# Three low parts of weights per layer made by GpSimd, and softmax divisions written as products of two tensors

## The chip, the core and the metric

The kernel runs on one core of a Trainium2 chip. The metric is the device time of one execution in microseconds, the median of several. The engines are TensorE (PE in the profile), VectorE (DVE), ScalarE (ACT), GpSimd (POOL) and SyncE (SP), which issues the loads of the weights. They run beside each other and wait for each other on semaphores.

## What is computed

Two transformer blocks of two layers each, on one sequence of 256 tokens and 1024 features, in fp32. The change lies in the heads of the first block's layers:

```python
def hybrid_layer(x, ...):
    proj = rms_norm(x, ln1) @ w_in
    ...
    y_moba = moba_attention(mq, mk, mv)      # 6 heads; causal softmax over 256 keys at this length
    ...
    h = mlstm_chunkwise(...)                 # 4 heads
    h = h * sigmoid(xo)
    y_mlstm = rms_norm(h, mlstm_norm)
    ...
    y_swa = swa_attention(sq, sk, sv, swa_sinks)   # 6 query heads, window 128, softmax with a sink
    x = x + concatenate([y_moba, y_mlstm, y_swa]) @ w_out
    u = rms_norm(x, ln2) @ w_up
    return x + square(relu(u)) @ w_down
```

## The kernel before

Every weight is multiplied as the sum of two parts in a short fp32 format, so that the product keeps its precision. The weights come in units of up to 128x1024 elements, two to a slab of 1 MB, in the order in which TensorE uses them. For each unit ScalarE writes the high part (`act_split`, line 377) and VectorE the low part, the weight less its high part (`dve_split`, line 386, a TENSOR_TENSOR with both inputs in SBUF). High and low parts lie in rings of RING = 4 buffers: unit u reuses the buffers of unit u - 4, and ScalarE waits until TensorE has used those. The semaphore `unit_lo` counts the low parts in the order of the units. TensorE waits on it before each unit (`pe_unit_in`), and SyncE before it overwrites a slab (three slab buffers).

Each engine has its own program in an order that is written out by hand. In a layer of the first block, five groups of projection columns come first. Then u0 is the number of the next unit, and a loop `for i in range(0, N1, 2)` runs over the 16 heads in pairs: heads 0 to 3 are mLSTM, 4 to 9 MOBA, 10 to 15 the windowed attention. Units u0 to u0+3 are the last column group (the values), u0+4 to u0+7 the first half of the output projection (a chunk pair each, consumed inside the loop from i = 8 on), u0+8 and later its second half.

One pass of the loop does, on TensorE: the transposes of the scaled probabilities of heads i and i+1 (line 1016, after `prob_ready`), the scores of heads i+4 and i+5 (line 1000), the products with the values of heads i-2 and i-1 (line 1048), and column products or chunks of the output projection (lines 420 to 422). At i = Y_TURN = 10 it also transposes the mLSTM output, after `y_ready`. On VectorE: `first` for heads i+4 and i+5 (line 1444: scores plus mask from PSUM, with the row maximum; these wait for the scores), at i = 10 the low part of the mLSTM output (line 1560), `seconds(i + 2)` (line 1457: the reciprocal of the sums, for the heads with a sink after adding the sink at line 1454; line 1460: four instructions that scale the probabilities of heads i+2 and i+3, of 128 and 256 columns a head), `pair(i - 2)` (line 1468), the low part of one weight unit, and at i = 4 and i = 6 the mLSTM output's normalisation (`y_first`, lines 1477 to 1483, and `y_mean`, lines 1489 and 1491). On ScalarE: copies of the transposes, high parts, the exponentials (line 887).

GpSimd follows the mLSTM output (`pool_layer1`): gate (line 1690), square (1693), then the wait for `y_mean`, the root (`root`, line 1658), a product with the root (1698) and one with the gain (1702), which sets `y_ready`.

Of the kernel before, what the change touches and what calls it, by code (L numbers as in the profile page):

```python
# [8 lines left out]
F32 = mybir.dt.float32  # L9
# [4 lines left out]
P = 128  # L14
# [12 lines left out]
MOBA, LSTM, SWA, SWA_KV = 6, 4, 6, 2  # L27
# [36 lines left out]
HALF = 1024  # L64
SLAB = 2 * HALF
RAW, RING = 3, 4
# [16 lines left out]
def wide_units(name, c0, w):  # L83

    n = HALF // w
    while DC % n or (DC // n) % 2:
        n -= 1
    return [[(name, k + i, c0, w) for i in range(n)] for k in range(0, DC, n)]


def tile_units(name, chunks, c0):

    return [[(name, k, c0, P) for k in range(a, min(a + DC, chunks))] for a in range(0, chunks, DC)]
# [3 lines left out]
G1 = [(0, ZLQ + LSTM * HD)]  # L97
# [4 lines left out]
def plan1():  # L102
    plan = []
    for c0, w in G1:
        plan += wide_units("w_in", c0, w)
    for k in range(0, DC, 2):
        plan.append([("w_out", c, n * P, P) for c in (k, k + 1) for n in range(OUT_HALF)])
    for n in range(OUT_HALF, DC):
        plan += tile_units("w_out", DC, n * P)
    for n in range(FC1):  # L110
        plan += tile_units("w_up", DC, n * P)
    for n in range(DC):
        plan += tile_units("w_down", FC1, n * P)
    return plan
# [26 lines left out]

PLAN = [(l, unit) for l in range(DEPTH) for unit in plan1()] + [(l, unit) for l in range(DEPTH) for unit in plan2()]
SLABS = len(PLAN) // 2
DOWN1, DOWN2 = len(tile_units("", FC1, 0)), len(tile_units("", FC2, 0))


def width_of(u):
    return sum(b[3] for b in PLAN[u][1])
# [26 lines left out]
def build(nc, a, out):  # L175
    ctx = ExitStack()
    with ctx:
# [16 lines left out]
        raw = [sb(f"raw{i}", [P, SLAB]) for i in range(RAW)]  # L194
        w_hi = [sb(f"w_hi{i}", [P, HALF], F32R) for i in range(RING)]
        w_lo = [sb(f"w_lo{i}", [P, HALF], F32R) for i in range(RING)]
# [30 lines left out]
        rinv = sb("rinv", [P, PROBS, T])  # L227
# [81 lines left out]
        prob = [work[:, i * GROUP:(i + 1) * GROUP] for i in range(PROBS)]  # L309
# [71 lines left out]
        def dve_split(dve, b, to):  # L381
            while b.made < min(to, len(PLAN)):
                u = b.made
                n, j = width_of(u), u // 2
                dve.wait_ge(s["unit_hi"], u + 1)
                nc.vector.tensor_tensor(w_lo[u % RING][:, 0:n], raw[j % RAW][:, (u % 2) * HALF:(u % 2) * HALF + n],  # L386
                                        w_hi[u % RING][:, 0:n].bitcast(F32), ALU.subtract).then_inc(s["unit_lo"], 1)
                b.made += 1

# [74 lines left out]
        def pool_squares(pool, b):  # L466

            k = b.at("rsum")
            for n in range(1, DC):
                pool.wait_ge(s["sq_ready"], k * DC + n + 1)  # L470
                if n > 1:
                    pool.wait_ge(s["sq_added"], k * (DC - 1) + n - 1)
                nc.gpsimd.tensor_tensor(sumsq[:, :], sumsq[:, :], sq[n % 2][:, :], ALU.add).then_inc(s["sq_added"], 1)
# [40 lines left out]
        def pool_norm(pool, b):  # L514
            n = b.mark("rsum")
            pool.wait_ge(s["ms_ready"], n)
            nc.gpsimd.tensor_tensor(rstd[:, :], ms2[:, :], half[:, 0:T], ALU.pow).then_inc(s["rstd_ready"], 1)  # L517
# [815 lines left out]
        def dve_layer1(dve, b, l, next_gain):  # L1333
# [115 lines left out]
            def seconds(i):  # L1449
                hd, p = HEADS1[i], i % PROBS  # L1450
                wait(dve, value(b, "exp_done", hd["n"] + 2))
                total = esum
                if hd["sink"] is not None:
                    tick(dve, b, dve_chain, nc.vector.tensor_tensor(tot[:, p:p + 2, :], esum[:, p:p + 2, :],
                                                                    esink[:, p:p + 2, :], ALU.add))
                    total = tot
                tick(dve, b, dve_chain, nc.vector.reciprocal(rinv[:, p:p + 2, :], total[:, p:p + 2, :]))
                for j in (p, p + 1):
                    for t in range(T):
                        ins = nc.vector.tensor_scalar(prob[j][:, HALVES1[t]], prob[j][:, HALVES1[t]],  # L1460
                                                      rinv[:, j, t:t + 1], None, ALU.mult)
                    ins.then_inc(s["prob_ready"], 1)

            def pair(i):
# [22 lines left out]
            def y_mean():  # L1487
                wait(dve, value(b, "y_sq", 1))
                tick(dve, b, dve_chain, nc.vector.tensor_reduce(ssq[:, m0:m1].rearrange("p (t h) -> p t h", t=T),
                                                                by_head(lstm_q[:, :, :]), X, ALU.add))  # L1490
                nc.vector.tensor_scalar(msq[:, m0:m1], ssq[:, m0:m1], 1.0 / HD, EPS, ALU.mult, ALU.add)\
                    .then_inc(s["qms_ready"], 1)
# [57 lines left out]
            for i in range(0, N1, 2):  # L1550
                if i == 0:
                    lstm_probs(2)
                    lstm_probs(3)
                if i + PROBS < N1:
                    first(i + PROBS)
                    first(i + PROBS + 1)
                if i == Y_TURN:
                    bank = f["y"][0]
                    wait(dve, value(b, "y_hi", 1))
                    nc.vector.tensor_tensor(act_b[:, 3:5, 1, :], tp[bank][:, :].rearrange("p (c s) -> p c s", s=S),  # L1560
                                            act_b[:, 3:5, 0, :].bitcast(F32), ALU.subtract).then_inc(s["y_lo"], 1)
                if LSTM <= i + 2 < N1:
                    seconds(i + 2)
                if i - 2 >= LSTM:
                    pair(i - 2)
                if i <= Y_TURN:
                    dve_split(dve, b, u0 + RING - 1 + i // 2)
                if i == LSTM:
                    y_first()
                if i == LSTM + 2:  # L1570
                    y_mean()
            dve_split(dve, b, u0 + RING + Y_TURN // 2 + 1)
            pair(N1 - 2)
            gain = pcol1[:, l, C_LN2:C_LN2 + DC]
# [58 lines left out]
            dve_down(dve, b, DOWN1, 1.0, act_a, next_gain)  # L1633

        def pool_layer1(pool, b, l):
            pool_norm(pool, b)
            if l == 0:
                pool.wait_ge(s["const_in"], 16 * n_const)
# [52 lines left out]
                .then_inc(s["y_gated"], 1)  # L1691
            wait(pool, value(b, "y_gated", 1))
            nc.gpsimd.tensor_tensor(lstm_q[:, :, :], lstm_h[:, :, :], lstm_h[:, :, :], ALU.mult).then_inc(s["y_sq"], 1)
            m0, m1 = R1_AT[2], R1_AT[2] + T * LSTM
            root(3, m0, m1)
            wait(pool, value(b, "qrs_ready", 3))
# [3 lines left out]
            wait(pool, value(b, "y_unit", 1))  # L1700
            g = prow1[:, l, R_MN:R_MN + LSTM * HD].unsqueeze(1).broadcast_to([P, T, LSTM * HD])
            nc.gpsimd.tensor_tensor(lstm_h[:, :, :], lstm_h[:, :, :], g, ALU.mult).then_inc(s["y_ready"], 1)
            pool_squares(pool, b)
            pool_norm(pool, b)
            layer_over(b, LAYER1)
# [540 lines left out]
```

## Time and profile before

| | us |
|---|---|
| Median of 3 runs | 1725.83 (1723.84 to 1726.46) |
| The profiled execution | 1721.79 |
| Its span, first to last instruction | 1720.0 |
| TensorE busy | 1672.9 (97%) |
| VectorE busy | 1257.4 (73%) |
| ScalarE busy | 991.0 (58%) |
| GpSimd busy | 147.3 (9%) |

TensorE's granted clock was 1.0 (2.4 GHz) throughout. In the rows, PE is TensorE's products and PEld its weight loads, L1460 is line 1460, `out<-in` are the program's names, and a time in square brackets is the engine's idle time before the row with what ended it. A timeline's row may stand for several like instructions (x4): its length then runs from the start of the first to the end of the last. Instructions of one engine overlap a little, so from start to start is shorter than the length. The first layer's head stage lies at 76 to 127 us, that of the second layer at 377 to 427.

### The profile page before, as it was taken

To read this page: it belongs to the slowest core of one execution; us is meant where nothing else is said; L and a number is where in the kernel's file an instruction comes from. 1 tells how busy PE (TensorE), PEld (TensorE's weight loads), DVE (VectorE), ACT (ScalarE), POOL (GpSimd) and SP (SyncE) were. 2 spreads that over 40 slices of the span, in tenths; PEclk is the share of its full clock that TensorE was granted. 3 is DMA by queue.
4 is the path that set the end of the run, shared out by engine and by line. 5 is a ranking of instruction groups with operands and counts; after the bars stand their busy time and mean duration, and the time that the engine had idled before them with its cause. 6 is when DMAs were issued, how large, how long until landed. Compare 5 with 4: busy or idle time off the path is not lost.

```text
span 1720.0 us, 25627 instructions
## 1 busy us (share of the span) xinstructions
PE 1672.9 (97%) x9966; PEld 1448.4 (84%) x9966; DVE 1257.4 (73%) x2025; ACT 991.0 (58%) x1664; POOL 147.3 (9%) x100
## 2 busy tenths in 40 slices
PE   7989999998999999999999999999999999999999
PEld 5778888877888888888877988888888787898888
DVE  7777766767776568876777878767886767778874
ACT  5666654567665455554566665545555466665552
POOL 2611000161100000001300000000000220000000
PEclk9999999999999999999999999999999999999999
DMA  7525555532655555556423455555556542355553
GB/s 283 190 99 184 196 197 196 219 136 99 233 196 200 195 193 196 187 205 245 172 99 123 178 190 196 193 201 194 188 183 217 208 183 99 139 181 196 183 203 129
DMA packets 62023, 313.99 MB, mean 183 GB/s; under 512 B 22685, under 2 KB 24353, under 8 KB 25294
## 3 DMA queue, kind: packets, MB, share of 16 engines
q1 hardware_dynamic: 60382, 303.93, 49.9%
q0 software_dynamic: 1232, 4.22, 0.8%
q10 hardware_dynamic: 288, 4.19, 0.6%
q8 instruction: 80, 1.31, 0.3%
q14 instruction: 41, 0.34, 0.1%
HBM read 311.25 MB, written 7.36 MB: 185 GB/s over the span
## 4 chain that ended last, share of the span: by engine, by line
PE 88%; DVE 6%; ACT 4%; issue 2%; DMA 0%; SPq 0%; ACTq 0%; DVEq 0%
PE acc L411 44%; PE acc L413 23%; PE acc L400 4%; PE acc L401 4%; PE acc L402 4%; DVE w_lo L386 2%; ACT w_hi L377 2%; PE acc L420 1%; PE acc L422 1%; PE acc L421 1%; PE sc L783 1%; PE acc L808 1%; PE tp L794 1%; ACT work L887 1%; PE tp L1016 1%
## 5 line engine op out<-in xcount | busy, mean ns | idle before, releaser
L386 DVE TENSOR_TENSOR w_lo<-raw,w_hi 128x1024 fp32r<-128x1024 f32 (+1 forms) x564 | 685.0, 1221 | 290.5 <-ACT w_hi L377 288.7
L377 ACT ACTIVATE w_hi<-raw 128x1024 fp32r<-128x1024 f32 (+1 forms) x564 | 584.1, 1039 | 194.2 <-PE acc L413 120.2
L411 PE MATMUL acc<-act_a,w_hi 128*128 128x512 f32 x1440 | 506.9, 396 | 1.2 <-DVE w_lo L386 1.2
L411 PE MATMUL acc<-hidden,w_hi 128*128 128x512 f32 x1216 | 421.8, 391 | 0.0
L413 PE MATMUL acc<-act_a,w_lo 128*128 128x256 f32 x1440 | 402.2, 279 | 0.0
L413 PE MATMUL acc<-hidden,w_lo 128*128 128x256 f32 x1216 | 340.0, 280 | 0.0
L411 PEld LDWEIGHTS acc<-act_a,w_hi 128*128 128x128 f32 x1440 | 269.7, 187 | 68.1 <-issue 8.5
L413 PEld LDWEIGHTS acc<-act_a,w_lo 128*128 128x128 f32 x1440 | 271.7, 189 | 0.1
L411 PEld LDWEIGHTS acc<-hidden,w_hi 128*128 128x128 f32 x1216 | 227.5, 187 | 50.3
L585 ACT COPY part<-acc 128x256 f32<-128x256 f32 x272 | 101.4, 373 | 270.9 <-PE acc L413 269.9
L411 PE MATMUL acc<-act_b,w_hi 128*128 128x512 f32 x688 | 239.4, 392 | 0.0
L413 PEld LDWEIGHTS acc<-hidden,w_lo 128*128 128x128 f32 x1216 | 229.6, 189 | 0.0
L413 PE MATMUL acc<-act_b,w_lo 128*128 128x256 f32 x688 | 192.7, 280 | 0.0
L411 PEld LDWEIGHTS acc<-act_b,w_hi 128*128 128x128 f32 x688 | 128.7, 187 | 28.3
L400 PE MATMUL acc<-w_hi,act_a 128*128 128x512 f32 (+2 forms) x352 | 135.2, 384 | 17.0 <-DVE w_lo L386 17.0
L401 PE MATMUL acc<-w_lo,act_a 128*128 128x512 f32 (+2 forms) x352 | 131.6, 374 | 0.0
L402 PE MATMUL acc<-w_hi,act_a 128*128 128x512 f32 (+2 forms) x352 | 131.6, 374 | 0.0
L413 PEld LDWEIGHTS acc<-act_b,w_lo 128*128 128x128 f32 x688 | 130.0, 189 | 0.1
L517 POOL TENSOR_TENSOR rstd<-ms,neg_half 128x2 f32<-128x2 f32 x10 | 12.5, 1251 | 1183.1 <-DVE ms L508 1183.1
L400 PEld LDWEIGHTS acc<-w_hi,act_a 128*128 128x128 f32 x352 | 67.3, 191 | 32.6 <-issue 15.5
L436 ACT ACTIVATE act_a<-x_res,pcol 128x256 fp32r<-128x256 f32 x64 | 31.8, 507 | 104.8 <-DVE x_res L599 92.5
L402 PEld LDWEIGHTS acc<-w_hi,act_a 128*128 128x128 f32 x352 | 67.3, 191 | 11.7
(210 smaller groups left out, 2043.8 us busy)
## 6 DMA issues: line engine op xcount, KB each, us to landing
raw<-in_slabs SPq DMA_DIRECT2D x282, 1024.0 KB, 4.8
na_skew<-in_rpb SPq DMA_DIRECT2D x32, 128.0 KB
na_bias<-na_skew ACTq DMA_DIRECT2D x2, 2048.0 KB, 8.6
t_skew<-t_by_distance POOLq DMA_DIRECT2D x2, 1024.0 KB, 14.3
t_bias<-t_skew POOLq DMA_DIRECT2D x1, 2048.0 KB, 10.7
x_res<-in_x SPq DMA_DIRECT2D x1, 1024.0 KB, 4.9
out_x<-x_res SPq DMA_DIRECT2D x8, 128.0 KB, 4.8
prow<-in_prow SPq DMA_DIRECT2D x1, 518.0 KB
```

Source lines behind the costliest of these rows:

```text
L377: nc.scalar.activation(w_hi[u % RING][:, 0:n], raw[j % RAW][:, (u % 2) * HALF:(u % 2) * HALF + n], ACT.Copy).then_inc(s["unit_hi"], 1)
L386: nc.vector.tensor_tensor(w_lo[u % RING][:, 0:n], raw[j % RAW][:, (u % 2) * HALF:(u % 2) * HALF + n], w_hi[u % RING][:, 0:n].bitcast(F32), ...
L400: nc.tensor.matmul(to, xh, wh, start=first and i == 0, stop=False)
L401: nc.tensor.matmul(to, xh, wl, start=False, stop=False)
L402: mm = nc.tensor.matmul(to, xl, wh, start=False, stop=last and i == n - 1)
L411: nc.tensor.matmul(bank[:, :], wh, src[:, c + i, :, :].rearrange("p i s -> p (i s)"), start=first and i == 0, stop=False, skip_group_check ...
L413: mm = nc.tensor.matmul(bank[:, S:2 * S], wl, src[:, c + i, 0, :], start=False, stop=last and i == n - 1, skip_group_check=True)
L420: nc.tensor.matmul(to, wh, src[:, c, 0, :], start=first, stop=False, skip_group_check=True)
L421: nc.tensor.matmul(to, wh, src[:, c, 1, :], start=False, stop=False, skip_group_check=True)
L422: return nc.tensor.matmul(to, wl, src[:, c, 0, :], start=False, stop=last, skip_group_check=True)
L436: nc.scalar.activation(to[:, n, 0, :], x[:, n, :], ACT.Identity, scale=gain[:, n:n + 1])\
L585: nc.scalar.copy(part[n % 2][:, :], acc[bank][:, 0:S]).then_inc(s["part_ready"], 1)
```

## The change

Three low parts per layer, of units u0+5, u0+6 and u0+7, are made by GpSimd (`pool_split`): u0+5 behind the square at line 1693 and ahead of the root, u0+6 and u0+7 behind the product with the gain. Each waits for its high part and for the low parts of all units ahead of it, so that `unit_lo` still counts in order. VectorE makes low parts in the loop for i up to 4 only; behind the loop it waits once for `unit_lo` (`dve_skip`) and goes on with u0+8. And the scaling of the probabilities is a TENSOR_TENSOR with the reciprocals broadcast over the columns in place of a TENSOR_SCALAR. It has two inputs in SBUF, in place of one and a scalar pointer. The diff:

```diff
--- before.py
+++ after.py
@@ -141,6 +141,7 @@
 
 PLAN = [(l, unit) for l in range(DEPTH) for unit in plan1()] + [(l, unit) for l in range(DEPTH) for unit in plan2()]
 SLABS = len(PLAN) // 2
+UNITS1 = len(plan1())
 DOWN1, DOWN2 = len(tile_units("", FC1, 0)), len(tile_units("", FC2, 0))
 
 
@@ -387,6 +388,20 @@
                                         w_hi[u % RING][:, 0:n].bitcast(F32), ALU.subtract).then_inc(s["unit_lo"], 1)
                 b.made += 1
 
+        def pool_split(pool, u):
+
+            n, j = width_of(u), u // 2
+            pool.wait_ge(s["unit_hi"], u + 1)
+            pool.wait_ge(s["unit_lo"], u)
+            nc.gpsimd.tensor_tensor(w_lo[u % RING][:, 0:n], raw[j % RAW][:, (u % 2) * HALF:(u % 2) * HALF + n],
+                                    w_hi[u % RING][:, 0:n].bitcast(F32), ALU.subtract).then_inc(s["unit_lo"], 1)
+
+        def dve_skip(dve, b, to):
+
+            while b.made < to:
+                b.made += 1
+            dve.wait_ge(s["unit_lo"], to)
+
 
 
         def columns_unit(u, src, c, banks, w, first, last):
@@ -1457,8 +1472,9 @@
                 tick(dve, b, dve_chain, nc.vector.reciprocal(rinv[:, p:p + 2, :], total[:, p:p + 2, :]))
                 for j in (p, p + 1):
                     for t in range(T):
-                        ins = nc.vector.tensor_scalar(prob[j][:, HALVES1[t]], prob[j][:, HALVES1[t]],
-                                                      rinv[:, j, t:t + 1], None, ALU.mult)
+                        w = HALVES1[t].stop - HALVES1[t].start
+                        ins = nc.vector.tensor_tensor(prob[j][:, HALVES1[t]], prob[j][:, HALVES1[t]],
+                                                      rinv[:, j, t:t + 1].broadcast_to([P, w]), ALU.mult)
                     ins.then_inc(s["prob_ready"], 1)
 
             def pair(i):
@@ -1563,12 +1579,13 @@
                     seconds(i + 2)
                 if i - 2 >= LSTM:
                     pair(i - 2)
-                if i <= Y_TURN:
+                if i <= LSTM:
                     dve_split(dve, b, u0 + RING - 1 + i // 2)
                 if i == LSTM:
                     y_first()
                 if i == LSTM + 2:
                     y_mean()
+            dve_skip(dve, b, u0 + RING - 1 + Y_TURN // 2)
             dve_split(dve, b, u0 + RING + Y_TURN // 2 + 1)
             pair(N1 - 2)
             gain = pcol1[:, l, C_LN2:C_LN2 + DC]
@@ -1633,6 +1650,7 @@
             dve_down(dve, b, DOWN1, 1.0, act_a, next_gain)
 
         def pool_layer1(pool, b, l):
+            u0 = l * UNITS1 + sum(len(wide_units("", c0, w)) for c0, w in G1[:G_V])
             pool_norm(pool, b)
             if l == 0:
                 pool.wait_ge(s["const_in"], 16 * n_const)
@@ -1691,6 +1709,7 @@
                 .then_inc(s["y_gated"], 1)
             wait(pool, value(b, "y_gated", 1))
             nc.gpsimd.tensor_tensor(lstm_q[:, :, :], lstm_h[:, :, :], lstm_h[:, :, :], ALU.mult).then_inc(s["y_sq"], 1)
+            pool_split(pool, u0 + RING + LSTM // 2 - 1)
             m0, m1 = R1_AT[2], R1_AT[2] + T * LSTM
             root(3, m0, m1)
             wait(pool, value(b, "qrs_ready", 3))
@@ -1700,6 +1719,8 @@
             wait(pool, value(b, "y_unit", 1))
             g = prow1[:, l, R_MN:R_MN + LSTM * HD].unsqueeze(1).broadcast_to([P, T, LSTM * HD])
             nc.gpsimd.tensor_tensor(lstm_h[:, :, :], lstm_h[:, :, :], g, ALU.mult).then_inc(s["y_ready"], 1)
+            for u in range(u0 + RING + LSTM // 2, u0 + RING - 1 + Y_TURN // 2):
+                pool_split(pool, u)
             pool_squares(pool, b)
             pool_norm(pool, b)
             layer_over(b, LAYER1)
```

## Rows read from the trace of the kernel before

**Rows 1.** The page: the chain that ended last, share of the span by engine.
```profile
PE 88%; DVE 6%; ACT 4%; issue 2%; DMA 0%; SPq 0%; ACTq 0%; DVEq 0%
```
**Rows 2.** TensorE's waits, 76 to 127 us, then 380 to 430: total, times, longest.
```profile
PE tp L1016 <- DVE work L1460: 4.9, 4, 1.6
...
PE tp L1016 <- DVE work L1460: 4.7, 4, 1.5
```
**Rows 3.** Timeline of TensorE, layer 1: start, length, line, operation, count, idle before it.
```profile
100.72 1.00 PE L1016 MATMUL tp<-ident,work 128*128 128x128 f32 x6 [1.51 <-DVE work L1460]
101.66 0.93 PE L1000 MATMUL sc<-heads_t 64*128 64x128 f32 x8
...
106.65 0.55 PE L1016 MATMUL tp<-ident,work 128*128 128x128 f32 x3 [1.63 <-DVE work L1460]
108.12 0.55 PE L1016 MATMUL tp<-ident,work 128*128 128x128 f32 x3 [0.93 <-DVE work L1460]
...
113.19 1.00 PE L1016 MATMUL tp<-ident,work 128*128 128x128 f32 x6 [0.85 <-DVE work L1460]
...
114.92 0.39 PE L420 MATMUL acc<-act_b,w_hi 128*128 128x256 f32 x1
```
**Rows 4.** Timeline of VectorE, layer 1.
```profile
100.12 1.01 DVE L1460 TENSOR_SCALAR work<-work,rinv 128x128 f32<-128x128 f32 x4
101.04 0.42 DVE L1468 TENSOR_TENSOR act_b<-acc,act_b 128x256 fp32r<-128x256 f32 x1
101.38 1.22 DVE L386 TENSOR_TENSOR w_lo<-raw,w_hi 128x1024 fp32r<-128x1024 f32 x1
...
103.71 0.35 DVE L1444 CUSTOM_DVE_ANT_0 work<-sc,mask_s,neg_sink 128x128 f32<-128x128 f32 x1 [0.32 <-issue]
...
105.47 2.59 DVE L1460 TENSOR_SCALAR work<-work,rinv 128x128 f32<-128x128 f32 x4
...
111.58 0.69 DVE L1560 TENSOR_TENSOR act_b<-tp,act_b 128x512 fp32r<-128x512 f32 x1 [0.47 <-ACT act_b L1279]
```
**Rows 5.** Timeline of GpSimd, layer 1.
```profile
80.42 2.36 POOL L1680 TENSOR_TENSOR qk<-qk,qk_b 128x1024 f32<-128x1024 f32 x1
...
98.87 1.04 POOL L1693 TENSOR_TENSOR lstm_q<-lstm_h 128x512 f32<-128x512 f32 x1
103.47 1.65 POOL L1658 TENSOR_TENSOR rstd_h<-msq,neg_half 128x8 f32<-128x8 f32 x1 [3.57 <-DVE msq L1491]
105.20 1.04 POOL L1698 TENSOR_TENSOR lstm_h<-lstm_h,rstd_h 128x512 f32<-128x512 f32 x1
106.32 1.39 POOL L1702 TENSOR_TENSOR lstm_h<-lstm_h,prow 128x512 f32<-128x512 f32 x1
```
**Rows 6.** Timelines: GpSimd and VectorE near 1361 us, VectorE near 72 and 60 us.
```profile
1361.04 9.01 POOL L2079 TENSOR_TENSOR na_bias<-mask_n,na_bias 128x4096 f32<-128x4096 f32 x1 [2.95 <-DMA na_bias<-na_skew]
...
1361.19 9.94 DVE L386 TENSOR_TENSOR w_lo<-raw,w_hi 128x1024 fp32r<-128x1024 f32 x1 [1.67 <-ACT w_hi L377]
...
72.55 0.67 DVE L1403 TENSOR_TENSOR qk<-z,rope_gc 128x384 f32<-128x384 f32 x1
...
59.82 1.49 DVE L1403 TENSOR_TENSOR qk<-z,rope_gc 128x384 f32<-128x384 f32 x3
```
**Rows 7.** Timeline of VectorE, near 375 us: a product of 128 columns.
```profile
374.85 0.28 DVE L1403 TENSOR_TENSOR qk<-z,rope_gc 128x128 f32<-128x128 f32 x1
```
**Rows 8.** Timelines of short stretches: single instructions of GpSimd and VectorE.
```profile
406.18 1.10 POOL L1698 TENSOR_TENSOR lstm_h<-lstm_h,rstd_h 128x512 f32<-128x512 f32 x1
406.30 1.13 DVE L1460 TENSOR_SCALAR work<-work,rinv 128x256 f32<-128x256 f32 x1
...
106.51 1.29 DVE L1460 TENSOR_SCALAR work<-work,rinv 128x128 f32<-128x128 f32 x1
```
**Rows 9.** Timelines of VectorE and TensorE, layer 2 of the first block.
```profile
404.33 0.35 DVE L1444 CUSTOM_DVE_ANT_0 work<-sc,mask_s,neg_sink 128x128 f32<-128x128 f32 x1
...
408.85 0.55 PE L1016 MATMUL tp<-ident,work 128*128 128x128 f32 x3 [0.82 <-DVE work L1460]
```

## Prediction

> **What bounds the kernel now.** I read the chain that ended last first [rows 1]: 88% of it is TensorE, so a change outside TensorE counts only where TensorE waits. Then the waits of TensorE in the heads' stage of each layer of the first block [rows 2]: of this change's neighbourhood nearly all of the waiting, 4.9 us in the first layer and 4.7 us in the second, is for the scaled probabilities of line 1460. Then the timelines of the stage. On TensorE [rows 3] one sees the transposes of heads 8 and 9 at 100.72, of 10 at 106.65, of 11 at 108.12 and of 12 and 13 at 113.19, each started by VectorE. On VectorE [rows 4]: head pair 8/9 scaled at 100.12, a weight unit's low part at 101.38 (two more follow, one after pair 10/11 and one after 12/13), the row maxima of heads 12 and 13 at 103.71, and pair 10/11 scaled at 105.47 in 2.59 us where pair 8/9 took 1.01. On GpSimd [rows 5]: the mLSTM output's square at 98.87, the root at 103.47, its two products at 105.20 and 106.32. Those 2.59 us lie exactly beside those products. The weight units are not late: the first moved one, u0+5, is wanted at 114.92 [rows 3].
>
> **Who holds whom.** In the second block's layer 2 a 128x4096 product on GpSimd starts at 1361.04 and takes 9.01; a VectorE low part that starts 0.15 later takes 9.94 instead of 1.22 [rows 4, 6]. It ran after GpSimd, not beside it: 1361.19 + 9.94 - 1.22 = 1369.91, or 0.14 ahead of GpSimd's end. That is a TENSOR_TENSOR with both inputs in SBUF, the form the divisions now take. A factor that is broadcast doesn't free the instruction: the 128x384 product with rope_gc, which is broadcast over the heads, took 0.67 at 72.55 beside GpSimd's last rope products, and three others of its shape 1.49, some 0.5 each [rows 6]. So I take it that GpSimd and a two-input VectorE instruction exclude each other for a whole instruction, and that who asks first goes first: GpSimd's 406.18 product slipped in behind one VectorE instruction, and the next, at 406.30, took 1.13 [rows 8].
>
> The Trainium skill, page SBUF — State Buffer, section Who interferes with whom, has this as a rule: tensor_tensor with two SBUF inputs contends with GpSimd's reads just as a 2-port tensor_scalar does, and the one that issues first blocks the other fully. It speaks against the new form being any cure, and the trace agrees by the 9.94 us.
>
> **Part 1, the form of the division.** Start to start, a product of 128 columns costs 0.21 (0.28 busy [rows 7]) and of 256 columns 0.34 (101.04 to 101.38 [rows 4, 7]): 1.10 for a pair of heads, where the tensor_scalars need 0.92 (100.12 to 101.04). So +0.09 for the first head and +0.18 for both, wherever a pair is on the path. Pairs 4/5 and 6/7 are covered by the column products of a value unit, which TensorE has ahead of either pair's transposes (lines 1130 and 1131); uncovered they would cost 0.18 each. The bounds of such a pair are +0.0 and +0.4 (its four instructions at 0.07 to 0.1 more each).
>
> The Trainium skill, page VectorE: DVE Perf Modes, section The perf-mode tier table, gives 1227 ns for a fp32 tensor_scalar of 2048 columns and 2293 ns for a tensor_tensor. By that the 384 columns of a head would cost 0.20 more, not 0.09, and an estimate by it would add some 0.1 to each layer; the rows of these very sizes are nearer.
>
> **Part 2, unit u0+5 on GpSimd, behind the square.** VectorE is rid of 1.22 [rows 4] between pair 4's low part and the mean at line 1489. GpSimd gains an instruction whose price no row has; the nearest is 128x1024 with two inputs, 2.36 [rows 5], and 9.01 / 4 = 2.25 bounds it below; if it must alternate with VectorE it grows by what it waits. I take 2.36. In layer 1 it is issued at 98.87 + 1.04 + 0.08, plus 0.18 for part 1: 100.17. VectorE starts its first product at 100.12, so GpSimd comes in behind it (100.33), and ends at 100.17 + 2.36 + 0.16 = 102.69, letting go 0.15 earlier. The three other products of pair 8/9 wait: head 8 is ready at 102.95 (before: 100.66), head 9 at 103.5 (101.13). Head 9's transpose, and with it the scores that start at 101.66, move by 2.37. The row maxima start 0.14 behind those scores' end: 104.96 + 0.14 = 105.1, where they started at 103.71: only +1.39, since they had waited for VectorE's low part and mean. Meanwhile VectorE does pair 4, the mean and the 128x8 msq (done 104.64, GpSimd idle), and the root runs from 104.72 to 106.37 with its 1.65.
>
> **Part 3, pair 10/11 and the order on the shared path.** From the maxima's start to the first product it is 1.76 (103.71 to 105.47 [rows 4]), so the products start at 106.86, inside GpSimd's product of 106.45 to 107.49 (1.04). Released at 107.32, two of them run (107.32, 107.53) before GpSimd's next, issued at 107.57; that one ends at 108.98 and the last two run to 109.44. Head 11 is transposed at 109.5 against 108.12: +1.38. In layer 2 [rows 9] the maxima started at 404.33 without a pause; scores moved by 2.35 bring them to 406.07 (+1.74), and the same steps give head 11 at 410.5 against 408.85: +1.65. The 1.6 us that the TENSOR_SCALARs lost beside GpSimd (2.59 against 1.01) are lost again, by products.
>
> **Part 4, units u0+6 and u0+7 on GpSimd, behind the gain.** Each takes 2.36: 109.1 to 111.7 and 111.8 to 114.2. VectorE saves two low parts, of which none was on the path (both lie in front of a wait for scores or beside TensorE's out-projection). What is on it is the sum, line 1454, of pair 12/13, two SBUF inputs: y's low part [rows 4] ends at 111.58 + 1.38 + 0.6 = 113.56, GpSimd lets go at 114.0: +0.44. With part 1's 0.18 layer 1 ends **2.0 us** later, layer 2 (+1.65, +0.43, +0.18) **2.26 us** later. From there TensorE has no wait on VectorE until its out-projection is done, and everything behind follows TensorE, so nothing is given back and nothing is added. VectorE's new wait, dve_skip, stands behind pair 12's low part, near 120, with units u0+8 and u0+9 queued behind it; u0+7 is done at 114.2, so it costs nothing. SyncE refills a slab on the same counter: 0.2 later for u0+5, earlier for the others, with units in hand.
>
> **The sum.** 2.0 + 2.26 = 4.3 us. The profiled execution took 1721.79 (span 1720.0), so 1726.1; the median of the runs is 1725.83, 4.04 above it, and the forecast is **1730.1 us**. A measurement of this kernel can tell about 0.2%, 3.45 us, from no change: the line lies at 1729.3.
>
> **The rivals.**
> 1. *GpSimd wins a close turn.* In part 3 VectorE's second product leads GpSimd's next by 0.04, and its fourth leads u0+6's by 0.05 or a little more. In the trace VectorE went first with a lead of 0.07 (the product at 106.51 took 1.29, so the one before it had got in [rows 8]), and lost with 0.01 in layer 2. If either is lost, u0+6's 2.2 us stand before the last product of head 11: +2.2, less the 0.4 of part 4, 1.8 a layer. Lost in one layer 1731.9, in both 1733.7. Chance 0.27.
> 2. *The products pass beside GpSimd* (the other side). If the broadcast factor is read so that the second path isn't used, nothing waits: maxima at 102.9, pair 10/11 done at 105.8, head 11 at 105.86 against 108.12, less 0.18: 2.1 us gained, and 1.85 in layer 2. 1721.9. It decides in favour of the change as soon as a pair beside GpSimd takes under 2.2 us: the 2.26 gained are then more than the excess over 1.1 of two pairs. Against it stand the 9.94 and the 0.67. Chance 0.09.
> 3. *GpSimd starts u0+5 late*, behind all four products of pair 8/9 (1.1 us later than worked out, by slow waits on two semaphores). Then it holds only the 128x8 msq: maxima at 103.7 as before, parts 3 and 4 cost a few tenths each. About 1727. For it: GpSimd's starts are rough. Chance 0.15.
>
> **How the numbers follow.** Forecast 0.45, rivals 0.27, 0.09, 0.15, the rest 0.04. The forecast's own spread is about 1 us (GpSimd's 2.25 to 2.5 four to six times over, the 0.0 to 0.4 of part 1), so nearly a third of it falls below 1729.3; with rival 1 that makes slower 0.61, with rival 3 same 0.29, faster 0.10. The range leaves out rival 2 and the far end of rival 1: 1726.5 to 1734.5.
>
> **What would show it.** Three low parts a layer on GpSimd at 2.4 us or more; three of the four products of pair 8/9 spread over 3.4 us, the second or third taking over 2; TensorE's wait before heads 8 and 9 grown from 1.5 to about 3.9; pair 10/11 over 2.3 us; the sum of pair 12/13 at 0.5 instead of 0.15. If pair 8/9 takes 1.1 us with GpSimd busy beside it, the whole argument falls, and rival 2 holds.

## The result, and the profile after

The kernel after the change takes 1738.05 us in the median of four runs (1737.09 to 1742.44), the kernel before 1725.07 in four runs beside it: 1.0082 times as long, 95% interval 1.0066 to 1.0097. The sign was as forecast. The size was not: 13.0 us between the medians where 4.3 were worked out, and above the upper end of the range, 1734.5. In the profiled execution it took 1742.44 (span 1740.6).

Totals and granted clock from the page of the kernel after; each digit of the clock is a fortieth of the span. Before, all forty digits were 9.

```profile
PE 1686.2 (97%) x9966; PEld 1458.4 (84%) x9966; DVE 1262.9 (73%) x2019; ACT 991.5 (57%) x1664; POOL 163.9 (9%) x106
...
PEclk9989999998999999999999999999999999999999
```

TensorE is busy 13.3 us more with the same 9966 products. That can't come from waiting: they ran at a lower clock. The 8s are the heads' stages of the two layers (the part of a layer in which the 16 heads' probabilities are made and used). Busy time by stretches of 5 us in layer 1's, with the granted clock in the third column from the end (before, it was 1.00 in all of them):

```profile
100.00:105.00 5.00, 3.16 (x16) 2.14 (x18) 3.42 (x7) 2.60 (x10) 2.77 (x2) 0.63 0.56 177
105.00:110.00 5.00, 3.86 (x20) 2.94 (x20) 4.75 (x11) 3.45 (x12) 4.83 (x4) 0.68 0.09 34
110.00:115.00 5.00, 2.33 (x12) 1.74 (x14) 3.49 (x5) 0.96 (x2) 2.54 (x1) 0.66 0.22 61
115.00:120.00 5.00, 4.78 (x28) 3.24 (x24) 2.48 (x12) 2.13 (x8) 0.00 (x0) 0.66 0.36 152
120.00:125.00 5.00, 4.42 (x36) 3.48 (x38) 3.23 (x12) 3.81 (x11) 0.00 (x0) 1.00 0.00 0
```

TensorE's waits in the same stage, 76 to 135 us, then 380 to 445 (before: 4.9 and 4.7 in total, longest 1.6 and 1.5 [rows 2]):

```profile
PE tp L1031 <- DVE work L1476: 8.3, 4, 3.7
...
PE tp L1031 <- DVE work L1476: 8.4, 4, 3.7
```

TensorE's timeline, layer 1 (the rows that answer to [rows 3]; lines have moved by 15):

```profile
101.84 1.54 PE L1031 MATMUL tp<-ident,work 128*128 128x128 f32 x6 [3.70 <-DVE work L1476]
103.32 1.65 PE L1015 MATMUL sc<-heads_t 64*128 64x128 f32 x8
...
110.53 0.55 PE L1031 MATMUL tp<-ident,work 128*128 128x128 f32 x3 [1.67 <-DVE work L1476]
113.21 0.90 PE L1031 MATMUL tp<-ident,work 128*128 128x128 f32 x3 [2.14 <-DVE work L1476]
...
120.58 1.08 PE L1031 MATMUL tp<-ident,work 128*128 128x128 f32 x6 [0.80 <-DVE work L1476]
```

The transposes of heads 8 and 9 follow a wait of 3.70 us and take 1.54 where they took 1.00; the scores behind them take 1.65 where they took 0.93. The clock recovers (head 10's transposes take 0.55 as before), and falls again with head 11's, 0.90 for 0.55, behind another wait of 2.14.

VectorE, layer 1 (answers to [rows 4]), and below it GpSimd (answers to [rows 5]):

```profile
99.05 3.28 DVE L1476 TENSOR_TENSOR work<-work,rinv 128x128 f32<-128x128 f32 x4
...
105.11 0.35 DVE L1459 CUSTOM_DVE_ANT_0 work<-sc,mask_s,neg_sink 128x128 f32<-128x128 f32 x1 [1.65 <-PE sc L1015]
...
106.69 1.00 DVE L1469 TENSOR_TENSOR tot<-esum,esink 128x4 f32<-128x4 f32 x1
...
107.93 5.22 DVE L1476 TENSOR_TENSOR work<-work,rinv 128x128 f32<-128x128 f32 x4
```
```profile
96.61 1.27 POOL L1708 TENSOR_TENSOR lstm_h<-lstm_h,z 128x512 f32<-128x512 f32 x1 [12.88 <-DVE lstm_h L1499]
97.96 1.04 POOL L1711 TENSOR_TENSOR lstm_q<-lstm_h 128x512 f32<-128x512 f32 x1
98.96 2.35 POOL L396 TENSOR_TENSOR w_lo<-raw,w_hi 128x1024 fp32r<-128x1024 f32 x1
103.54 1.65 POOL L1676 TENSOR_TENSOR rstd_h<-msq,neg_half 128x8 f32<-128x8 f32 x1 [2.23 <-DVE msq L1507]
105.26 1.04 POOL L1717 TENSOR_TENSOR lstm_h<-lstm_h,rstd_h 128x512 f32<-128x512 f32 x1
106.39 1.28 POOL L1721 TENSOR_TENSOR lstm_h<-lstm_h,prow 128x512 f32<-128x512 f32 x1
107.62 5.05 POOL L396 TENSOR_TENSOR w_lo<-raw,w_hi 128x1024 fp32r<-128x1024 f32 x2
```

The two engines hold each other up: an instruction of the one waits until one of the other is over. I call that the lock below. Pair 8/9 stands for 3.28 us beside u0+5 (98.96 to 101.31), pair 10/11 for 5.22 (layer 2: 6.04) beside u0+6 and u0+7 (107.62 to 112.67), and the sum with the sink, 0.16 us when free, takes 1.00 beside the product with the gain. The single rows of pair 10/11 show who holds whom: its first product, asked for 0.31 after u0+6 began, ends 0.15 behind it, and so does its third with u0+7 (110.13 to 112.67).

```profile
107.93 2.20 DVE L1476 TENSOR_TENSOR work<-work,rinv 128x128 f32<-128x128 f32 x1
```

In layer 2 the sum passes (0.16), and the pair meets GpSimd one instruction earlier. Its first product is held by the product with the gain (0.87), and when that ends, u0+6 is ahead of its second:

```profile
415.95 1.10 POOL L1721 TENSOR_TENSOR lstm_h<-lstm_h,prow 128x512 f32<-128x512 f32 x1
417.01 2.40 POOL L396 TENSOR_TENSOR w_lo<-raw,w_hi 128x1024 fp32r<-128x1024 f32 x1
```
```profile
417.13 2.56 DVE L1476 TENSOR_TENSOR work<-work,rinv 128x256 f32<-128x256 f32 x1
```

Not every GpSimd instruction holds VectorE. Its root (a power of few elements) doesn't, in the kernel before already: beside an earlier root of layer 1 two low parts, with two inputs in SBUF each, take their usual 1.21 us.

```profile
58.34 5.11 POOL L1658 TENSOR_TENSOR rstd_h<-msq,neg_half 128x24 f32<-128x24 f32 x1 [5.11 <-DVE msq L1393]
```
```profile
61.23 2.35 DVE L386 TENSOR_TENSOR w_lo<-raw,w_hi 128x1024 fp32r<-128x1024 f32 x2
```

To compare runs whose stages begin at slightly different times, I count from the start of GpSimd's gate product, the first of its rows above (96.61; before, 97.51). In layer 1, against before, the transposes of head 8 come 2.02 us later, the maxima of heads 12 and 13 2.30, the first product of pair 10/11 3.36, head 11's transposes 5.99 and those of heads 12 and 13 8.29. (Ahead of the gate product VectorE scales a pair in the new form, 0.16 longer; against TensorE's own work each of these is 0.16 more.) GpSimd's first sum of squares for the norm, the end of the stage, comes 39.08 us after the gate product, before 30.72: **8.36 us** in layer 1, 38.72 against 30.43, **8.29**, in layer 2. I call this distance the stage's length below.

Why 16.7 us in the traces are 13.0 in the medians: the clock also falls for a few microseconds at places that have nothing to do with the change, now here, now there. The profiled execution of before had none (clock 1.000, 1721.79). In the last batch of experiments before ran 29 times: its five runs at a mean clock of 1.000 took 1721.6 to 1722.5, the six at 0.999 took 1722.4 to 1722.8, the six at 0.998 1724.4 to 1725.7, the twelve at 0.996 1726.3 to 1728.6. After's profiled run had falls at 820 to 860 and 1460 to 1500 (0.97, 0.95, 0.92, 0.91 of 20 us each: 5.0 us), and without them would, by this estimate, stand at 1737.4, like its other three (1737.1 to 1738.5). From clean run to clean run the change costs 15 to 16 us. That is 16.7 less 0.9, by which its gate product came earlier in layer 1.

### The profile page after: what moved, and what is told of

It is laid out like the page before. It is cut to its first block, busy times and chain, and to the rows that moved or that the text cites. A ratio compares the mean times of both kernels' runs of the same rounds, so it can differ in the third digit from the quotient of the medians.

```text
span 1740.6 us, 25635 instructions
## 1 busy us (share of the span) xinstructions
PE 1686.2 (97%) x9966; PEld 1458.4 (84%) x9966; DVE 1262.9 (73%) x2019; ACT 991.5 (57%) x1664; POOL 163.9 (9%) x106
## 4 chain that ended last, share of the span: by engine, by line
PE 88%; DVE 6%; ACT 4%; issue 1%; DMA 0%; SPq 0%; DVEq 0%; ACTq 0%
PE acc L426 44%; PE acc L428 23%; PE acc L415 4%; PE acc L417 4%; PE acc L416 4%; DVE w_lo L387 3%; ACT w_hi L378 2%; PE acc L435 1%; PE acc L437 1%; PE acc L436 1%; DVE work L1476 1%; PE sc L1015 1%; PE acc L823 1%; PE tp L1031 1%; PE sc L798 1%
```

## The experiments

All ratios are against runs of the kernel before on the same chip. The stage's length is given for both layers.

**The form alone.** Before, with the divisions as TENSOR_TENSORs:

```diff
-                        ins = nc.vector.tensor_scalar(prob[j][:, HALVES1[t]], prob[j][:, HALVES1[t]],
-                                                      rinv[:, j, t:t + 1], None, ALU.mult)
+                        w = HALVES1[t].stop - HALVES1[t].start
+                        ins = nc.vector.tensor_tensor(prob[j][:, HALVES1[t]], prob[j][:, HALVES1[t]],
+                                                      rinv[:, j, t:t + 1].broadcast_to([P, w]), ALU.mult)
```

> The kernel before with the divisions as products of two tensors and nothing else. Theory L (a GpSimd instruction and a VectorE instruction with two SBUF inputs exclude each other for a whole instruction, as GpSimd and TENSOR_SCALAR do): pair 10/11 still takes 2.5 to 2.8 us beside GpSimd's two products, the others 1.16 instead of 1.01; the time is 1725.1 plus 0.2 to 1.0. Rival F (the new form escapes GpSimd): pair 10/11 takes 1.2 us, the time falls by about 2.8, to 1722.3.

Measured: 1725.73 us in ten runs, ratio 1.0003 (0.9990 to 1.0016). Pair 10/11 takes 2.85 us in layer 1 and 2.91 in layer 2, where before had 2.59 and 2.70, and the other pairs 1.16. The stages are 31.15 and 32.35, +0.43 and +1.92, the second with a fall of the clock on the path. The form escapes nothing and costs little; it is neither a cure nor the main cause.

**The units alone.** After, with the divisions of before:

```diff
-                        w = HALVES1[t].stop - HALVES1[t].start
-                        ins = nc.vector.tensor_tensor(prob[j][:, HALVES1[t]], prob[j][:, HALVES1[t]],
-                                                      rinv[:, j, t:t + 1].broadcast_to([P, w]), ALU.mult)
+                        ins = nc.vector.tensor_scalar(prob[j][:, HALVES1[t]], prob[j][:, HALVES1[t]],
+                                                      rinv[:, j, t:t + 1], None, ALU.mult)
```

> The changed kernel with the divisions as TENSOR_SCALAR again: the three units on GpSimd alone. Theory L: TENSOR_SCALAR is held by the units just as the products are, so within 2 us of the changed kernel, 1736 to 1740, with pair 8/9 over 3 us and pair 10/11 over 5. Rival F (it is the form that is dear when it meets GpSimd): under 1730.

Measured: 1737.08 in four runs, 1.0063 (1.0044 to 1.0081). Pair 8/9 takes 2.89, pair 10/11 4.92 and 4.93, a little less than expected. The first product alone takes 2.17 for 0.28: the plain TENSOR_SCALAR is held as well. The stages are 37.69 and 38.23, and of the 16.7 us that the change adds to the two all but 1.9 are the units.

**Only u0+5 on GpSimd, and only u0+6 and u0+7.** After, with the other low parts back on VectorE. The first:

```diff
-                if i <= LSTM:
+                if i == LSTM + 4:
+                    dve_skip(dve, b, u0 + RING - 1 + LSTM // 2 + 1)
+                if i <= Y_TURN and i != LSTM + 2:
                     dve_split(dve, b, u0 + RING - 1 + i // 2)
...
-            dve_skip(dve, b, u0 + RING - 1 + Y_TURN // 2)
...
-            for u in range(u0 + RING + LSTM // 2, u0 + RING - 1 + Y_TURN // 2):
-                pool_split(pool, u)
```

> The changed kernel with only unit u0+5 on GpSimd. Theory L: pair 8/9 takes 3.3 us as in the changed kernel, pair 10/11 some 2.5 to 3.5 (only GpSimd's two products are there), TensorE's clock falls once a layer; about 2.5 to 3.5 a layer above before, 1730 to 1732. If the harm comes from u0+6 and u0+7 alone: 1725 to 1726.

The second:

```diff
-                if i <= LSTM:
+                if i <= LSTM + 2:
                     dve_split(dve, b, u0 + RING - 1 + i // 2)
...
-            pool_split(pool, u0 + RING + LSTM // 2 - 1)
```

> The changed kernel with only units u0+6 and u0+7 on GpSimd. Theory L: pair 8/9 takes 1.2 us, pair 10/11 5 to 6, and head 11 is some 4 us late; with one fall of the clock 4.5 to 5.5 a layer above before, 1734 to 1736. If the harm comes from u0+5 alone: 1725 to 1726.

Measured: 1728.11 in ten runs, 1.0017 (1.0005 to 1.0029), and 1731.65 in six, 1.0041 (1.0023 to 1.0059). Stages: 32.83 and 32.20 with u0+5, +2.11 and +1.77; 35.49 and 34.74 with the other two, +4.77 and +4.31. Both expectations were too high. With u0+5 alone the sum and pair 10/11 come so late that GpSimd's products are over or nearly so (0.98 for the sum in layer 1, 0.86 for the first product in layer 2), and the pair takes 1.17 and 1.74. With the other two it takes 5.00 and 5.05. The parts add up to 6.9 and 6.1 of the 8.4 and 8.3: together they cost more. That the later maxima of the one run into the longer GpSimd work of the other is how I read it.

Single rows of the second kernel, layer 1: VectorE's last two products of pair 10/11, and GpSimd.

```profile
106.14 1.35 DVE L1476 TENSOR_TENSOR work<-work,rinv 128x128 f32<-128x128 f32 x1
...
107.42 2.56 DVE L1476 TENSOR_TENSOR work<-work,rinv 128x256 f32<-128x256 f32 x1
```
```profile
105.82 1.53 POOL L1720 TENSOR_TENSOR lstm_h<-lstm_h,prow 128x512 f32<-128x512 f32 x1
...
107.31 2.39 POOL L396 TENSOR_TENSOR w_lo<-raw,w_hi 128x1024 fp32r<-128x1024 f32 x1
```

This is the second close turn of the prediction, with nothing ahead of the pair disturbed. The low part begins at 107.31, the product with the gain ends at 107.35 by its row: GpSimd begins 0.04 *before* its own predecessor is over, and 0.11 ahead of VectorE's fourth product, which then takes 2.56 instead of 0.4. Layer 2 of this kernel loses it in the same way (2.56).

**GpSimd's units behind the pairs.** After, each low part held back until the pair beside it is scaled:

```diff
+            wait(pool, value(b, "prob_ready", 6))
             pool_split(pool, u0 + RING + LSTM // 2 - 1)
...
-            for u in range(u0 + RING + LSTM // 2, u0 + RING - 1 + Y_TURN // 2):
+            for u, ready in ((u0 + RING + LSTM // 2, 8), (u0 + RING + LSTM // 2 + 1, 10)):
+                wait(pool, value(b, "prob_ready", ready))
                 pool_split(pool, u)
```

> The changed kernel with GpSimd's three low parts behind waits on the pairs of heads: u0+5 starts when pair 8/9 is scaled, u0+6 when 10/11 is, u0+7 when 12/13 is. The same work on the same engines, but none lies beside the products that it held. Theory L: pair 8/9 takes 1.2 us, pair 10/11 2.5 (GpSimd's two products still hold it), 12/13 1.2; the time returns to within 2 us of before, 1724 to 1727. If GpSimd's work costs in another way (its speed, late units): stays above 1732.

Measured: 1727.13 in ten runs, 1.0009 (0.9994 to 1.0024). Pair 8/9 takes 1.16 again, pair 10/11 3.08 and 2.91, near the 2.85 and 2.91 of the form alone. The same low parts on the same engine, u0+5 1.3 us later, u0+6 at the same time but with the pair already scaled, u0+7 4.3 and 3.0 us later: and 11 of the 13 us between the medians are gone, 12.9 of 16.7 by the stages. So it is the meeting that costs, not the work. What is left is such a meeting too: the sum with the sink of pair 14/15 is asked for beside u0+7 and takes 2.23 and 2.22 (stages 33.14 and 31.75). The sum of pair 10/11 passes beside GpSimd's root (0.15).

**Idle transposes against the falling clock.** After, with transposes of the identity on TensorE ahead of the turns in which it waits, with `FILL = {8: 30, 10: 12, 11: 18}`:

```diff
+                if FILL.get(i):
+                    wait(pe, before)
+                    for _ in range(FILL[i]):
+                        nc.tensor.transpose(tp[bank][:, 0:P], ident[:, :], ident[:, :])
```

> The changed kernel with 30, 12 and 18 extra transposes of the identity on TensorE ahead of its waits for heads 8, 10 and 11, into the bank that the head's own transposes then overwrite; no one reads them. The holds on VectorE stay. Theory C (TensorE's granted clock falls to its lower level after these waits, and that costs as much as part of the holds themselves): the clock stays at 1.0, a layer takes some 3 us less than in the changed kernel, 1731 to 1733. If the clock costs nothing of the time: 1738 or more, since the extra transposes can only delay.

Measured: 1738.31 in four runs, 1.0081 (1.0060 to 1.0102). Heads 8 and 9 are transposed in 1.08, and the maxima behind them come 1.16 and 1.05 earlier than in the kernel after. But pair 10/11 then meets GpSimd at a worse place, 6.41 and 6.23 us, head 11 comes 0.96 and 1.24 later, and the clock falls all the same near head 11. The stages are 37.99 and 37.69, only 1.1 and 1.0 shorter than after's. The expectation failed, and as a test of the whole price of the clock it was badly made: it moved the two things at once. So I made it again where nothing ahead of the pair can move. In the kernel with only u0+6 and u0+7 on GpSimd, `FILL = {10: 12, 11: 24}`:

> The kernel with only units u0+6 and u0+7 on GpSimd, plus idle transposes of the identity on TensorE ahead of the turns of head 10 (12) and head 11 (24), where TensorE waits 1.77 and 3.20 us at full clock in that kernel. They change nothing on VectorE or GpSimd before head 11. Theory (the fall of the granted clock costs time of its own): the clock stays at 1.0, turn 11 takes 0.55 instead of 0.90, scores 0.93 instead of 1.66, turn 12 comes about 2 us earlier after head 11, and the whole is 1.5 to 2.5 us a layer shorter than the 1731.65 of that kernel: 1727 to 1728.5. Rival (the slow clock is covered by VectorE's path, or the chip takes its slow stretch elsewhere): turn 12 earlier by under 0.5 us, or the time within 1 us of 1731.65.

and in the kernel after, `FILL = {10: 8, 11: 16}`:

> The kernel after, with idle transposes ahead of head 10 (8) and head 11 (16) only, not ahead of head 8. Up to head 10's turn nothing can change, so the order of the two engines on pair 10/11 stays, which the run with fillers before head 8 did not keep. If the clock's second fall costs what theory says, 1.5 to 2.3 us a layer come back: 1733.5 to 1735 instead of 1738. If the clock's fall after the first wait lasts in spite of the fillers, or comes back elsewhere, 1737 to 1738.5.

TensorE and VectorE, layer 1, in the second of them:

```profile
111.84 1.91 PE L1027 MATMUL tp<-ident 128*128 128x128 f32 x16
114.16 0.55 PE L1036 MATMUL tp<-ident,work 128*128 128x128 f32 x3 [0.41 <-DVE work L1481]
114.64 0.93 PE L1016 MATMUL sc<-heads_t 64*128 64x128 f32 x8
```
```profile
99.98 3.26 DVE L1481 TENSOR_TENSOR work<-work,rinv 128x128 f32<-128x128 f32 x4
```

Head 11 comes where it came before the fillers (16.63 after the gate product against 16.60), but at full clock, 0.55 for 0.90, and its scores take 0.93 for 1.65; heads 12 and 13 then come 2.19 earlier (21.78 against 23.97). The stages are 36.89 and 36.55, **2.19 and 2.17 us** shorter than after's. In the other kernel they are 33.35 and 33.36, 2.14 and 1.38 shorter; in its layer 2 the fillers themselves hold head 11's transposes back by 0.44. The medians say less than this, 1737.14 in six runs (1.0070, 1.0055 to 1.0086) and 1730.91 in twelve (1.0031, 1.0020 to 1.0043), and both miss what was expected. Falls elsewhere are in most of these runs: the profiled one of the latter kernel, 1733.35, had four outside the heads, and less 1.8 for each it would be at 1726. Of that kernel's twelve runs the three at a mean clock of 1.000 took 1726.6 to 1726.9, just under the expected 1727 to 1728.5, against 1730.3 at best without fillers; of the other's six the two at 0.998 took 1734.4 and 1734.6, against 1737.1 at best. I take the price from the stages, and leave open whether a fall that is avoided here makes one elsewhere more likely; twelve and six runs don't tell.

**A division that GpSimd doesn't hold.** In the kernel before the maxima (line 1444) run beside GpSimd unhindered. What they have and the divisions haven't is a second result, a value per row (they also read their scores from PSUM, so this alone shows nothing). So: before, with a TENSOR_SCALAR that also writes the sum of its row to a tile that nobody reads.

```diff
+        rsum = sb("rsum", [P, PROBS, T])
...
                         ins = nc.vector.tensor_scalar(prob[j][:, HALVES1[t]], prob[j][:, HALVES1[t]],
-                                                      rinv[:, j, t:t + 1], None, ALU.mult)
+                                                      rinv[:, j, t:t + 1], 0.0, ALU.mult, ALU.add,
+                                                      accum_out=rsum[:, j, t:t + 1])
```

> The kernel before with the scaling as a TENSOR_SCALAR that also writes out its sum (to columns that no one reads). Theory L says that what is held is a form that reads SBUF on two paths; this form has one input and, if it reads it on one path only, passes beside GpSimd: pair 10/11 takes 1.3 to 1.7 us instead of 2.6, and the time falls by 1.5 to 2.5, to 1722.6 to 1723.6. If it is held as the others are: 1725.1 to 1726.5.

VectorE and GpSimd of that kernel, layer 1, at pair 10/11:

```profile
104.94 0.34 DVE L1461 TENSOR_SCALAR_CACHE_REDUCE work<-work,rinv 128x128 f32<-128x128 f32 x1
105.21 0.08 DVE L1461 DVE_READ_ACCUMULATOR work<-work,rinv 128x1 f32 x1
105.21 0.47 DVE L1461 TENSOR_SCALAR_CACHE_REDUCE work<-work,rinv 128x256 f32<-128x256 f32 x1
...
105.88 0.47 DVE L1461 TENSOR_SCALAR_CACHE_REDUCE work<-work,rinv 128x256 f32<-128x256 f32 x1
```
```profile
105.04 1.05 POOL L1700 TENSOR_TENSOR lstm_h<-lstm_h,rstd_h 128x512 f32<-128x512 f32 x1
```

Measured: 1722.19 in ten runs, 0.9981 (0.9967 to 0.9995): by this interval a little faster than before, and faster than after. The pair takes 1.4 us beside GpSimd where it took 2.59 and 2.70; in the trace of the stage all twelve instructions of a size take the same (mean 344 and 475 ns). TensorE waits before heads 8 and 12 only, and the stage is 29.75 in both layers: 0.97 and 0.68 shorter than before's, 1.65 in all. The medians are further apart because fifteen of the 25 runs of before beside it stand at a mean clock of 0.996 or less, and three of these ten. At 1.000 its two runs took 1720.7 and 1720.9, the eight of before 1721.1 to 1722.4.

The same division in the kernel after, with all three units on GpSimd:

> The changed kernel with the same summing TENSOR_SCALAR in place of the products of two tensors. If that form passes beside GpSimd, the units on GpSimd hold nothing but the short sum of pair 12/13 and the 128x8 msq, and VectorE is rid of a low part ahead of the mean: pair 8/9 and 10/11 under 1.7 us each, 1721 to 1724. If it is held: 1736 to 1740.

Measured: 1724.71 in ten runs, 1.0003 (0.9991 to 1.0016), just above the expected range, 13 us less than after and nothing lost against before. Stages 31.69 and 29.95. Both pairs take 1.4. What GpSimd still holds is the sum with the sink of pair 12/13, a TENSOR_TENSOR of four columns: 1.34 and 1.16 beside u0+7, with a wait of TensorE of 2.26 and 2.07 behind it, and in layer 1 the clock fell once more (heads 12 and 13 transposed in 1.55).

With that division and fewer units: only u0+5 on GpSimd, then u0+5 and u0+6.

> Only unit u0+5 on GpSimd, and the divisions as TENSOR_SCALARs that also write their sum, which GpSimd doesn't hold. Theory: pairs 8/9 and 10/11 in 1.4 us beside GpSimd, nothing on the path meets a GpSimd instruction, TensorE without a wait before heads 8 to 11 above 1.8 us, so that it ends like the kernel before with the same divisions (1722.2), or up to 1 us ahead of it because VectorE's low part no longer stands before the maxima: 1721 to 1722.5. Rival (the low part on GpSimd holds the low part of pair 4 and the mean, and the root and the two products then come later): 1723 to 1725.

> Units u0+5 and u0+6 on GpSimd, u0+7 on VectorE, divisions with their sum. In the run with all three units the sum with the sink of pair 12/13 was asked for 12.5 us after the gate product and held 1.34 us by u0+7; u0+6 ends at about 11.3. Theory: the sum takes 0.16, turn 12 comes 1 us earlier than there, and the time is 1721 to 1722.5 instead of 1724.7. Rival: VectorE's own u0+7 comes in front of that sum or of the maxima and costs its 1.22: 1723.5 to 1725.

Measured: 1721.83 in twelve runs, 0.9991 (0.9978 to 1.0004), and 1722.81 in twelve, 0.9988 (0.9978 to 0.9998). Stages 29.98 and 29.99 in the one, 29.99 and 29.98 in the other. As expected the sum of pair 12/13 takes 0.15 without u0+7 on GpSimd. But with u0+5 and u0+6 moved heads 12 and 13 come only 0.3 and 0.1 us earlier than with all three units, where 1 was expected, the median lies above the expected 1721 to 1722.5, and neither kernel's stage is shorter than the 29.75 with no unit moved: with u0+5 moved the sum of pair 10/11 meets a GpSimd product (0.90, 0.60; 1.04, 1.05 us). In the kernel with all three it was asked for within 0.01 us of that product's start and passed (0.16), and head 10 was transposed 1.1 us earlier than with no unit moved (7.77 against 8.84 after the gate product). With u0+5 and u0+6 it was asked for 0.01 to 0.02 after that start, and held: this kernel's stage hangs, as I read it, on a close turn that was lost. In these runs moving units brings nothing and the division does; that no placement of them could gain isn't shown.

## Why the prediction was wrong in size

Two steps failed. The prediction priced only the lock and put TensorE's clock at nothing: its two falls cost 1.1 and 2.3 us a layer. And in part 3 it took pair 10/11 to last 2.6 us, where it lasted 5.22 and 6.04, and left out the sum ahead of it. What follows takes it part by part.

**Who holds whom: right where it was used.** In the heads' stage every product of a division that was asked for inside one of GpSimd's products or low parts ended with it or up to 0.28 us behind (2.40 and 2.20 us for 0.28), and the kernel with GpSimd's units behind the pairs takes most of the cost away. As a rule for every GpSimd instruction it is too wide: the root holds nothing. The three products of 59.82 [rows 6] that the prediction took for unheld ran beside a root.

**Part 1, the form: right.** 1.17 for a pair against 1.01, 0.16 where 0.18 was put; alone it can't be told from no change.

**Part 2: right as a sum, one detail and one step wrong.** Head 8 came 2.18 later (2.02 and the 0.16), 2.29 were worked out. u0+5 took 2.35 where 2.36 was assumed, but it began with the square's end and stood ahead of all four products, not three; my 0.08 from one GpSimd instruction to the next was read from pairs in which the second needs the first. Then the maxima: +1.39 worked out, +2.46 measured. The step that failed here is the move of the scores by 2.37: they moved by 2.72, for the transposes ahead of them were slow (+0.35), and took 1.65 instead of 0.93 (+0.72), together the 1.07 that are missing. In layer 2 it is +2.76 for +1.74.

**Part 3: the largest miss.** For head 11 it had +1.38 and +1.65; the rows show +6.15 and +6.08, again with the pair ahead. Three terms. The clock's first fall gave 1.07 (above). In layer 1 the sum with the sink was held 0.84 (1.00 for 0.16), a two-input instruction on the path that the prediction counted for pair 12/13 and forgot for 10/11; with the maxima, 0.2 longer as well for a reason that I can't name, the first product came 1.06 later after them. In layer 2 the sum was not held. And the pair took 5.22 and 6.04, where before had 2.59 and 2.70 and some 2.6 were put: +2.63 and +3.34. It came so late that it met both low parts. Of the two close turns on which the forecast stood (leads of 0.04 and 0.05) the one against u0+6 arose in layer 2 of the kernel after, where VectorE's second product lost it (417.13 against 417.01), and in both layers of the kernel with u0+6 and u0+7 alone, where the fourth did. In layer 1 of the kernel after VectorE was too late for either. Rival 1 (chance 0.27) thus had the right place and the right loser. Its price was near too: without part 2 it gives 2.0 + 1.8 - 1.4 = 2.4 a layer, and the stage of that kernel with fillers is 2.63 and 2.93 longer than before's. Without fillers it is 4.77 and 4.31. The lock was priced; the clock behind it wasn't.

**Part 4: wrong.** "From there TensorE has no wait" held, and the sum of pair 12/13 was not held (0.44 had been put). But from head 11 to head 12 2.3 us were added, nearly all of them the clock's second fall, as the fillers show by giving 2.2 back.

**The forecast's base.** It added 4.04 us, the distance of before's median to its profiled run, as if it belonged to every run. By the mean clocks it was the price of falls elsewhere; in most of after's runs they were few or absent. This made the miss look smaller: 16.7 us of traces against 4.3 forecast, but 13.0 of medians.

By term, layer 1, from TensorE's own work on: the lock on pair 8/9 behind its slack 1.4 as forecast, the clock's first fall 1.1, the sum and pair 10/11 1.06 + 2.63 = 3.7 (of it the 0.2 of the longer maxima not shown to be the lock), the second fall 2.3: 8.5, which is the 8.36 and the 0.16. The 1.1 is read off the rows, and the run with fillers ahead of head 8 agrees: its maxima come 1.16 and 1.05 earlier. The second fall is isolated by the fillers, the lock by the units alone, singly and behind the pairs.

**Both forms of the division.** The Trainium skill, page SBUF — State Buffer, section Who interferes with whom, says that a VectorE instruction with two SBUF inputs contends with a GpSimd instruction that reads SBUF. The rows agree for GpSimd's products and low parts (2.40 us for 0.28); its root reads SBUF too and held nothing (1.21 us for each of two low parts beside it), and there the measurement decides. The same section excepts from the contention the tensor_scalar "that also writes out its accumulator". The traces agree: 0.34 and 0.47 us beside GpSimd's products, the same as without.

## What to carry to other kernels

Work that is moved to an idle GpSimd can cost VectorE's two-input instructions and its plain TENSOR_SCALARs its whole length if they meet, and by who asks first; look for every such instruction on the path, the four-column ones too, before moving anything, and don't rest a forecast on leads of some hundredths of a microsecond. If an instruction on the path can be given a form that isn't held (here a TENSOR_SCALAR that also writes its row's sum), that was worth more here than moving its neighbours. And price a longer wait of TensorE at more than its length: read in the granted clock what comes behind it.

## What the runs showed that I had not expected

- TensorE's granted clock falls from the higher of its two levels (2.4 GHz) to the lower (1.2 GHz) behind waits of 2.14 to 3.70 us in this stage. Products then take 1.5 to 1.8 times as long (1.54 for 1.00, 1.65 for 0.93). The second such fall of the kernel after cost 2.2 us of the stage; idle transposes in the wait took it away. The length of the last wait alone doesn't settle it: behind waits of 1.5 and 1.6 the profiled kernel before showed none, while with the form alone the clock fell behind one of 1.59 in layer 1, and in layer 2 behind one of 0.89 that followed one of 1.64 (0.90 for 0.55; that stage was 32.35 against 31.15 in layer 1). Where a wait for VectorE follows, a fall can cost nothing: the stage of 29.75 has one.
- The clock also falls at places that no edit touched, with about 1.8 us for each (0.91 over 20 us). They spread the runs of an unchanged kernel over 1721.6 to 1728.6 us, and are more than most edits here bring.
- GpSimd's low part starts up to 0.05 us before the end that the trace gives its predecessor, where the two share no data; with a wait between them it was 0.08 to 0.14 after.
- GpSimd's root (a power, 128x8 in 1.65 us, 128x24 in 5.11) doesn't hold VectorE's two-input instructions: 1.21 for a low part and 0.15 for the sum beside it, as without.
- A TENSOR_SCALAR in fp32 that also writes its sum costs 0.34 and 0.47 us for 128 and 256 columns, 1.4 a pair against 1.01 alone, and isn't held by GpSimd (1.4 against 2.59 and more).
